# Two of four weight sums made by transfers: a filled buffer and an accumulating DMA in place of one GpSimd addition

## What is computed

```python
x = x + jnp.einsum('bsd,de->bse', merged, w_out[l])
hf = rmsnorm(x, norm_ffn[l])
act = jax.nn.silu(jnp.einsum('bsd,df->bsf', hf, w_gate[l])) * jnp.einsum('bsd,df->bsf', hf, w_up[l])
x = x + jnp.einsum('bsf,fd->bsd', act, w_down[l])
```

## Time and profile before

| | us |
|---|---|
| median of three runs | 1755.92 |
| the runs | 1755.33, 1756.76, 1755.92 |
| the profiled execution, its own time | 1755.32 |
| its span | 1753.5 |
| PE busy | 1732.6 |
| DVE busy | 995.3 |
| ACT busy | 794.2 |
| POOL busy | 173.3 |

### The profile page before, as it was taken

One profiled execution on the slowest core, in us unless ns is written; L12 is line 12 of the kernel. 1 busy time (PEld: TensorE's weight loads), 2 busy tenths in 40 slices (PEclk: granted clock), 3 DMA queues, 4 the chain that ended last, 5 costly groups with the idle time before them and its releaser, 6 DMA issues.

```text
span 1753.5 us, 21136 instructions
## 1 busy us (share of the span) xinstructions
PE 1732.6 (99%) x7817; PEld 1434.9 (82%) x7817; DVE 995.3 (57%) x749; ACT 794.2 (45%) x706; POOL 173.3 (10%) x109
## 2 busy tenths in 40 slices
PE   9999999999999999999999989999999999999997
PEld 7888888888888888888888868888888888888886
DVE  5454455556565545444445466777777777544445
ACT  6444444445454433333334545444444445444444
POOL 1000010100000000000000023222322221000000
PEclk9999999999999999999999999999999999999999
DMA  8656655555555555655556545555555555555552
GB/s 288 194 171 191 190 164 174 168 167 180 165 182 192 194 193 190 194 189 193 190 192 216 192 148 203 198 194 191 192 195 197 198 198 195 213 191 191 191 193 94
DMA packets 152106, 331.09 MB, mean 189 GB/s; under 512 B 8736, under 2 KB 8832, under 8 KB 146048
## 3 DMA queue, kind: packets, MB, share of 16 engines
q1 hardware_dynamic: 152064, 330.51, 56.6%
HBM read 328.38 MB, written 2.10 MB: 188 GB/s over the span
## 4 chain that ended last, share of the span: by engine, by line
PE 96%; DVE 1%; POOL 1%; ACT 1%; issue 0%; DMA 0%; SPq 0%; DVEq 0%; POOLq 0%; ACTq 0%
PE ps L1342 18%; PE ps L1343 18%; PE ps L1351 18%; PE ps L1619 9%; PE ps L1620 9%; PE ps L1624 9%; PE ps L1689 4%; PE ps L1696 4%; PE ps L1691 4%; PE ps L1360 1%; PE ps L1580 1%; ACT w_hi L499 0%; DVE w_lo L884 0%; POOL t_raw L477 0%; DMA w_raw<-in_w_in 0%
## 5 line engine op out<-in xcount | busy, mean ns | idle before, releaser
L884 DVE TENSOR_TENSOR w_lo<-w_raw,w_hi 128x2048 fp32r<-128x2048 f32 x308 | 732.8, 2381 | 500.9 <-ACT w_hi L499 498.9
L499 ACT ACTIVATE w_hi<-w_raw 128x2048 fp32r<-128x2048 f32 (+1 forms) x309 | 589.5, 1911 | 447.3 <-PE ps L1343 214.0
L1342 PE MATMUL ps<-w_hi,xT_hi 128*128 128x512 f32 x1024 | 404.5, 395 | 0.9 <-ACT w_hi L499 0.9
L1343 PE MATMUL ps<-w_hi,xT_lo 128*128 128x512 f32 x1024 | 398.7, 389 | 0.0
L1351 PE MATMUL ps<-w_lo,xT_hi 128*128 128x512 f32 x1024 | 253.0, 389 | 0.0
L1342 PEld LDWEIGHTS ps<-w_hi,xT_hi 128*128 128x128 f32 x1024 | 192.3, 188 | 41.1 <-ACT w_hi L499 1.1
L1351 PEld LDWEIGHTS ps<-w_lo,xT_hi 128*128 128x128 f32 x1024 | 192.2, 188 | 39.9
L1343 PEld LDWEIGHTS ps<-w_hi,xT_lo 128*128 128x128 f32 x1024 | 192.4, 188 | 39.0
L1619 PE MATMUL ps<-w_hi,fT_hi 128*128 128x512 f32 x440 | 173.8, 395 | 7.6 <-DVE w_lo L884 7.3
L1620 PE MATMUL ps<-w_hi,fT_lo 128*128 128x512 f32 x440 | 171.7, 390 | 0.0
L477 POOL TENSOR_TENSOR t_raw<-w_raw 128x1024 f32<-128x1024 f32 x22 | 56.1, 2552 | 821.4 <-DVE form_lo L1197 532.8
(11 more groups left out here) (220 smaller groups left out, 1728.7 us busy)
## 6 DMA issues: line engine op xcount, KB each, us to landing
w_raw<-in_w_in SPq DMA_DIRECT2D x127, 1024.0 KB, 5.5
w_raw<-in_w_gate SPq DMA_DIRECT2D x88, 512.0 KB, 3.6
w_raw<-in_w_up SPq DMA_DIRECT2D x88, 512.0 KB, 4.4
w_raw<-in_w_down SPq DMA_DIRECT2D x44, 1024.0 KB, 4.8
w_raw<-in_w_branch_a SPq DMA_DIRECT2D x16, 1024.0 KB, 5.1
w_raw<-in_w_branch_b SPq DMA_DIRECT2D x16, 1024.0 KB, 5.0
w_raw<-in_w_out SPq DMA_DIRECT2D x16, 1024.0 KB, 5.1
xn<-in_x SPq DMA_DIRECT2D x4, 512.0 KB, 8.4
```

The lines of the kernel that those rows point to most:

```text
L499: copy = lambda o, i, **kw: nc.scalar.activation(o, i, ACT.Copy, **kw)
L884: V.tensor_tensor(w_lo[:, chunk.split, :], w_raw[:, chunk.raw, :], w_hi[:, chunk.split, :].bitcast(F32), ALU.subtract).then_inc(lo_split, 1)
L1342: T.matmul(ps[:, banks + r, :], rows(hi, k, r), w, start=(q == 0 and k == 0), stop=False)
L1343: last = T.matmul(ps[:, banks + r, :], rows(lo, k, r), w, start=False, stop=False)
```

## The change

In a summed step SP now loads unit 1 (`w_gate`, first half) into `t_raw[0]` and unit 2 (`w_up`, second half) into `t_raw[1]`, in two loads of 256 KB, beside the ordinary load of the whole block. POOL issues an accumulating DMA, which adds unit 0 (`w_up`, first half) from HBM to both, and waits for it. The first of the three additions goes; the other two stay. `form_raw0` moves from the bytes of `t_raw` to those of `t_lo`, and the wait for `form_lo` moves from POOL to DVE. SP takes over POOL's wait for `t_lo`.

```diff
-        form_raw0 = at("form_raw0", [P, 12, P], F32, s + 2 * HALF_CH)
+        form_raw0 = at("form_raw0", [P, 12, P], F32, s + HALF_CH)
...
-        T_STEPS = 3
+        T_STEPS = 2
...
             def load_pair(i):
                 for j in range(2 * BC):
                     c = Chunk(G_FFN + j, i, 2 * BC)
+                    if STEPS[j] == "S":
+                        if starts(i) and j == 0:
+                            sp.wait_ge(lo_split, c.count(1 - RAW_SLOTS))
+                        else:
+                            sp.wait_ge(t_lo_done, S_BEFORE[j] + i * S_TURNS)
+                        for n, (w, h) in enumerate(((w_gate_k, 0), (w_up_k, 1))):
+                            sp.dma_start(t_raw[:, n, :], halves(w)[:, h, PAIR_OF[j], bass.ds(i * COLS, COLS)]).then_inc(
+                                t_filled, 16)
                     sp.wait_ge(lo_split, c.count(1 - RAW_SLOTS))
                     for u, w in ((1, w_gate_k), (0, w_up_k)):
...
                 raw = raw_units[:, c.raw]
+                pool.wait_ge(t_filled, before * 32 + 32)
+                upper = w_up_k.rearrange("p (h k) n -> p h k n", h=2)[:, 0:1, PAIR_OF[j], bass.ds(i * COLS, COLS)]
+                nc.gpsimd.dma_start(out=t_raw[:, 0:2, :], in_=upper.to_broadcast([P, 2, COLS]),
+                                    accum_op=ALU.add).then_inc(t_summed, 16)
+                pool.wait_ge(t_summed, before * 16 + 16)
                 pool.wait_ge(pair_landed[c.raw], 32 * (j // RAW_SLOTS + 1) + i * 64)
-                if starts(i) and j == 0:
-                    pool.wait_ge(form_lo_done, 1)
-                else:
-                    pool.wait_ge(t_lo_done, before)
-                nc.gpsimd.tensor_tensor(out=t_raw[:, 0:2, :], in0=raw[:, 0:1, :].to_broadcast([P, 2, COLS]),
-                                        in1=raw[:, 1:3, :], op=ALU.add).then_inc(t_step, 1)
-                pool.wait_ge(t_step, before * T_STEPS + 1)
                 nc.gpsimd.tensor_tensor(out=raw[:, 0, :], in0=t_raw[:, 0, :], in1=raw[:, 2, :],
                                         op=ALU.add).then_inc(t_step, 1)
-                pool.wait_ge(t_step, before * T_STEPS + 2)
+                pool.wait_ge(t_step, before * T_STEPS + 1)
...
                 before = S_BEFORE[j] + i * S_TURNS
+                if starts(i) and j == 0:
+                    dve.wait_ge(form_lo_done, 1)
                 dve.wait_ge(t_hi_done, before + 1)
```

More of the change, by code:

```diff
@@ L295, in hybrid_block @@
         silu_done = sem("silu_done")
+        t_filled, t_summed = sem("t_filled"), sem("t_summed")
         a_hi_staged, a_lo_staged = sem("a_hi_staged"), sem("a_lo_staged")
```

## The result

| | us |
|---|---|
| before, median of three | 1755.92 |
| the change, median of three | 1773.25 (1771.27 to 1775.21) |
| ratio | 1.010, 95% interval 1.0084 to 1.0116 |
| profiled execution of the change, its own time | 1771.27, span 1769.5 |

What follows compares the result with a forecast made beforehand. PE was taken as the bound, busy 1732.6 of 1753.5 us. First-turn gain 5.0 less 0.7 for the clock gave 4.3, later turns 0: 1751.6 us, with a range of 1747.3 to 1759.

Steps and rivals of the forecast that it cites:

- Part 1, step 0 at 1018: Start of the first turn's step 0: PE's gap shrinks by 6.9 us, full clock saves 1.5, together 8.4.
- Part 2, step 3 of the first turn: Transfer not hidden before step 3: PE waits 3.6 us, first-turn gain 5.0, less 0.7 for the clock, net 4.3.
- X: Time of the accumulating transfer from POOL's issue to its semaphore: taken as 6.0 us, with ends of 3.6 and 10.
- Part 3, the later turns: The ten turns after the first: neither summed step nor the added loads make PE wait, 0 us.
- Sum: 0: Total for the ten turns after the first: no time gained or lost.
- No cost: Step 0 of later turns: fills go out well before its block, and the transfer overlaps the block's landing.
- the slack of step 3: Step 3 of later turns: the transfer may take up to 12.0 us before PE waits.
- every turn waits for step 3: Rival, chance 0.13: transfer from 12 us up delays step 3 in later turns; at 15 us, 1791 us.
- The extra traffic: Summed steps read 1 MB more each from HBM, 22 MB on 331, DMA share 56.6%: no wait.
- the transfer eats the gain: Rival, chance 0.26: transfer of 7 to 11 us, PE waits 4.7 to 8.7 in first-turn step 3; 1752.6 to 1757.4.

Runs made afterwards that it cites:

- e1: The kernel before with only form_raw0 moved into the bytes of t_lo, all sums on POOL, no fills or transfer: 1749.37 us, ratio 0.9966.
- e9: e1 with POOL's sums of step 3 put ahead of the norm's factor in the first turn, no transfer: 1747.34 us, ratio 0.9948.
- e8: The change, with SP loading step 3's block ahead of the wait for t_lo and the fills: 1755.00 us, ratio 0.9989 against the kernel before.
- e5: The change, with POOL's DMA copying instead of adding, so sums are wrong: 1752.45 us, ratio 0.9977 against the kernel before.
- e2: The change, with fills and transfer in step 0 alone, step 3 summed on POOL: 1756.53 us, ratio 1.0001 against the kernel before.
- e3: The change, with fills and transfer in step 3 alone, step 0 summed on POOL: 1756.04 us, ratio 0.9999 against the kernel before.
- e7: e1 plus an unused 256 KB load of w_up by SP in each of the 88 steps: 1751.99 us, ratio 0.9977 against the kernel before.
- e4: The change, with SP's fills for the next turn's step 0 ahead of the load of step 7: 1755.17 us, ratio 0.9993 against the kernel before.
- e11: The change itself run again without an edit: 1775.55 us, ratio 1.0114 against the kernel before.
- e6: The change, with POOL's DMA adding to the first row of t_raw alone, so sums are wrong: 1751.08 us, ratio 0.9970 against the kernel before.

## Why the prediction was wrong, by its steps

**Part 1, step 0 at 1018: right.** 6.9 less idle time and 1.5 from the clock were forecast. In the change the gap was 1.00, in e1 0.42, and the matmuls behind it ran at full clock (0.47 in the row at 1020.39, against 0.76 in the earlier trace rows). POOL's first transfer took 6.4 us, hidden as said. The output projection ended 0.9 us later in this execution than in that of before (1019.39 against 1018.46). That is no effect of the transfers: in e1 and e9, which have none, it ended at 1018.12 and 1019.78.

**Part 2, step 3 of the first turn: right in mechanism, net gain too high by 1.5.** Forecast was 11.0 - X with X = 6.0, and a wait of 3.6 us. Here the timeline of POOL, the place of the earlier trace rows:

```profile
1027.47 1.24 POOL L443 TENSOR_TENSOR r_x<-sums,half 128x2 f32<-128x2 f32 x1
1028.67 1.24 POOL L483 DMA_DIRECT2D t_raw<-in_w_up  x1
1035.02 1.39 POOL L487 TENSOR_TENSOR w_raw<-t_raw,w_raw 128x512 f32<-128x512 f32 x1 [5.11 <-DMA t_raw<-in_w_up]
```

X is 6.35, the wait 3.88. The clock did fall behind it (0.79 in the row at 1041.14), so its price is nearer to the 1.5 than to the 0.7 that I took. PE stood 1.8 us ahead of the kernel before at the transposes of the second turn (1079.32 against 1081.15), and 2.8 if one counts from the end of the projection. Forecast was 4.3. The terms as measured: 6.3 less at the start (7.30 to 1.00) and 1.5 from the clock, less 3.6 more waiting before step 3 (0.25 to 3.88) and about 1.5 for the clock behind it, 2.7.

**Part 3, the later turns: this step failed.** It said "Sum: 0", from X up to 12.0 before PE waits. Three things in it were wrong.

First, it took one X. The 6.0 held beside 1 MB of block loads or less; in step 3 of the later turns X was 9.6 to 10.4. The step had itself put the loads of step 3's and step 4's blocks into the same few microseconds, 2 MB, and sized the transfer by a row of 1 MB alone (e8 and e5 show what each does).

Second, for step 0 it said "No cost", as the fill goes out well before the block. It did, but behind step 7's wait for `w_lo` (3.9 us) and its 1 MB, and it took 6.2 us (1219.68 to POOL's DMA at 1225.84) where I counted 3.6 for such fills; then X up to 10.6. The sums of step 0, the part that was to gain, ended later than before, and `t_lo` with them.

Third, and this is the error of reasoning: the slack of step 3 was measured from the trace of before, with `t_lo` of step 0 at a fixed place, 5.5 us ahead of step 0. In the change `t_lo` has moved (SP's fill right behind it goes out at 1195.84 in one turn, 2.7 us ahead of a step 0 that starts at about 1198.5), because the step that ends with it runs the same chain. In that turn the slack of 12.0 is 12.0 - 2.8 (`t_lo` later) - 0.4 (a fill of 4.0) + 0.7 (sums of 2.7, not 3.3), about 9.4; X was 9.9, and PE waited 0.68. Each leg was compared with a fixed deadline, and each alone nearly fits, as e2 and e3 show; the sum of both around the shared buffer was never formed. It is 46.8 against 43.13 in the round shown. The two waits that close the loop were both in the text of the change (SP's for `t_lo`, and the load of step 7 ahead of the fill). The rival "every turn waits for step 3" had half of the place, and priced it as X above 12; it happens at 10. Five of the ten waits, 4.8 of 11.6 us, are before step 3; the other five, 6.9 us, are before step 0, where the prediction said "No cost" and no rival looked.

The step also put the landing of step 3's block near 1200; it landed at 1204.0, which cost nothing, as POOL's transfer ended later still (1209.7).

**The extra traffic: right in the later turns.** e7 shows no wait from it there.

**The rival "the transfer eats the gain"** had an X of 7 to 11, which the later turns have and step 3 of the first turn (6.35) has not. Its reason, POOL slowed beside DVE while it writes the issue, does not show: POOL was busy for 1.18 to 1.40 us at each of the 22 issues of the change. Adding and sharing account for the length (e5, e8).

## What to carry to other kernels

When two steps take turns in one buffer, add up everything from one refill to the next refill of the same buffer, all the way round, and compare that with the period; a slack read from the trace of before at one point of the loop says nothing once the other point moves. A chain of fill, transfer and semaphore that hangs on one loader's queue is also as long as whatever the loader issued just ahead of it: here the order of two small loads was worth 18 us. And try the parts of a change apart: moving one scratch buffer gave the gain, the transfer only cost. A loop of transfers that just fits is not safe either: here it fitted for three turns, then its transfers met other loads, grew, and it fitted no more.

## What the runs showed of the hardware that was not expected

An accumulating DMA of 512 KB takes 6.0 to 6.4 us from POOL's issue to its next instruction with at most 1 MB of block loads issued beside it (the first three transfers of the change; 6.0 to 7.2 in e8), about 10 with 2 MB. The same as a copy takes 4.4 to 5.9 and 7.1 to 8.3 in the same places (e5). The Trainium skill (DMA: Bandwidth & Descriptors, Anatomy of one DMA) fits 2.0 us plus bytes over 436 GB/s, an estimate of 3.2 us. These runs disagree for the accumulating form, whose least was 6.0, and the measurement decides; the copy's least, 4.4, is above it too, but no run here has it with nothing beside it. An added packet took (3.7% of 16 x 1769.5 us) / 5984 = 0.175 us of a DMA engine, one of SP's queue (57.8%) / 158400 = 0.103, and the adding transfer had 272 packets where the copy had 144. A copied packet of POOL's queue took (1.8% of 16 x 1752.3 us) / 3168 = 0.159 us (e5), nearly as much as an added one: what grew with the adding is mostly the number of packets, for the same bytes.

The clock of PE does not follow from the length of a wait alone. It fell to its lower level behind waits of 2.00, 2.43 and 3.88 us in the change, 2.55 in e7 and 5.18 in e4, but not behind 2.35 in e11 or 3.00 in e6 (the row at 1039.71 has 0.50, not 0.8):

```profile
1039.71 0.50 PE L1628 MATMUL ps<-w_hi,fT_hi 128*128 128x512 f32 x1 [3.00 <-ACT w_hi L506]
```

What decides it was not settled here.
